# Router on unnormalised rows in halves, row splits on POOL, two sets of transposes moved

## The reference, cut to what matters

```python
# first block
o = o * rsqrt(mean(o * o) + eps)                  # retention, per head
y_ret = (silu(g_ret) * o) @ w_branch_ret
mixed = sigmoid(gate_a) * y_ret + sigmoid(gate_b) * y_lru
h = h + mixed @ w_out
u = rmsnorm(h, ffn_norm_w);  gu = u @ w_ffn_in
# second block
mem_h = _rmsnorm(mem, g_mem);  k = _rmsnorm(mem_h @ w_kv[:, :1024] per head, k_gain)
x = x + merged @ w_out
h = _rmsnorm(x, g_ffn)                            # h = x * rsqrt(mean(x*x)+eps) * g_ffn
g_logits = h @ w_r1 + b_r1;  e_logits = h @ w_r2 + b_r2
g_sel = argmax(g_logits)                          # one of 4 groups per row
# in the group: the best 2 of 4 experts, softmax weights, hidden of 256, summed back
x = x + moe(h)
```

## Time and profile before

| | us |
|---|---|
| median of 3 runs | 1151.18 (1149.7 to 1153.47) |
| profiled execution | 1144.04 |
| its span, first to last instruction | 1142.1 |
| TensorE busy | 1105.1 (97%) |
| VectorE busy | 731.5 (64%) |
| ScalarE busy | 618.5 (54%) |
| POOL busy | 64.8 (6%) |

### The profile page before, as it was taken

How to read it: one execution, slowest core, us unless ns; L and a number is a source line. 1 busy time by engine, 2 the same in 40 slices (tenths; PEclk the granted TensorE clock), 3 DMA queues, 4 the chain that set the end, 5 groups by cost and what they waited for, 6 DMA issues and landing times.

```text
span 1142.1 us, 17273 instructions
## 1 busy us (share of the span) xinstructions
PE 1105.1 (97%) x7128; PEld 980.8 (86%) x7128; DVE 731.5 (64%) x809; ACT 618.5 (54%) x724; POOL 64.8 (6%) x56
## 2 busy tenths in 40 slices
PE   8999999999999999999999999899999989899996
PEld 5998889999878999998897778699999858688885
DVE  6854665865555444546765568956453677988884
ACT  7543479662455344434645355854434357777772
POOL 0410200000100000000000000000011100000140
PEclk9999999999999999999999999999999999999998
DMA  8552254654554555554454434234555535899891
GB/s 305 171 187 88 75 189 164 238 174 159 207 206 156 188 188 196 195 194 147 147 190 143 148 111 148 78 144 148 197 185 182 187 148 181 332 355 350 323 347 63
DMA packets 30468, 215.07 MB, mean 188 GB/s; under 512 B 3377, under 2 KB 3505, under 8 KB 4929
## 3 DMA queue, kind: packets, MB, share of 16 engines
q1 hardware_dynamic: 28112, 199.61, 49.5%
q0 software_dynamic: 1872, 13.11, 3.0%
q10 hardware_dynamic: 416, 1.39, 0.3%
HBM read 213.04 MB, written 1.05 MB: 187 GB/s over the span
## 4 chain that ended last, share of the span: by engine, by line
PE 86%; DVE 8%; ACT 3%; issue 1%; DMA 0%; POOL 0%; DVEq 0%; SPq 0%; ACTq 0%; POOLq 0%
PE bank L526 26%; PE bank L528 26%; PE bank L527 26%; DVE wlo L1511 1%; ACT buf L1040 1%; PE bank L1014 1%; PE bank L587 1%; PE bank L939 1%; DVE wlo L1508 1%; ACT whi L1040 1%; PE bank L900 1%; PE bank L882 1%; DVE normedT_lo L1535 0%; PE bank L651 0%; DMA buf<-x_dram 0%
## 5 line engine op out<-in xcount | busy, mean ns | idle before, releaser
L1511 DVE TENSOR_TENSOR wlo<-raw,whi 128x2048 fp32r<-128x2048 f32 x139 | 320.7, 2312 | 213.6 <-ACT whi L1040 213.3
L1040 ACT ACTIVATE whi<-raw 128x2048 fp32r<-128x2048 f32 x168 | 320.8, 1915 | 140.4 <-PE bank L528 140.1
L1040 ACT ACTIVATE buf<-bank 128x512 f32<-128x512 f32 (+5 forms) x167 | 78.8, 510 | 192.1 <-PE bank L528 171.4
L526 PE MATMUL bank<-normedT_hi,whi 128*128 128x256 f32 x640 | 179.2, 280 | 3.3 <-DVE normedT_lo L1535 3.3
L527 PE MATMUL bank<-normedT_lo,whi 128*128 128x256 f32 x640 | 178.3, 279 | 0.0
L528 PE MATMUL bank<-normedT_hi,wlo 128*128 128x256 f32 x640 | 178.2, 278 | 0.0
L526 PE MATMUL bank<-xT_hi,whi 128*128 128x256 f32 (+1 forms) x448 | 127.8, 285 | 3.2 <-DVE xT_lo L1556 3.2
L528 PE MATMUL bank<-xT_hi,wlo 128*128 128x256 f32 (+1 forms) x448 | 127.6, 285 | 0.0
L527 PE MATMUL bank<-xT_lo,whi 128*128 128x256 f32 (+1 forms) x448 | 127.4, 284 | 0.0
L526 PEld LDWEIGHTS bank<-normedT_hi,whi 128*128 128x128 f32 x640 | 120.9, 189 | 4.5 <-issue 4.1
L528 PEld LDWEIGHTS bank<-normedT_hi,wlo 128*128 128x128 f32 x640 | 121.5, 190 | 0.0
(11 more groups left out here) (383 smaller groups left out, 2277.0 us busy)
## 6 DMA issues: line engine op xcount, KB each, us to landing
raw<-weights_dram SPq DMA_DIRECT2D x168, 1024.0 KB, 4.9
buf<-weights_dram SPq DMA_DIRECT2D x19, 1024.0 KB, 5.1
buf<-x_dram SPq DMA_DIRECT2D x2, 512.0 KB, 4.3
buf<-mem_dram ACTq DMA_DIRECT2D x1, 1024.0 KB, 9.7
out_dram<-buf SPq DMA_DIRECT2D x2, 512.0 KB, 3.0
buf<-final_w_dram POOLq DMA_DIRECT2D x1, 512.0 KB, 3.9
con<-consts_dram SPq DMA_DIRECT2D x1, 486.0 KB, 10.0
buf<-small_w_dram SPq DMA_DIRECT2D x1, 432.0 KB, 12.5
```

The source lines that it names most:

```text
L526: E.matmul(out_, lh, rh, start=start, stop=False)
L1040: return S.activation(out_, in_, func, **kw)
L1511: V.tensor_tensor(wlo[:, n % SLOTS, :], raw[:, n % SLOTS, :], whi[:, n % SLOTS, :].bitcast(f32), sub).then_inc(piece_split, 1)
```

## The change

- The router's weights in `small_w` are multiplied by `gffn` once at the start. X itself is turned (`turn_out`) and split without scale or gain; each row's scale is applied to its 20 logits where the bias is added.
- X is added, squared and turned by column half c and row block r: t3.0 and t3.1 (the left half) are turned between out2's matmuls, t3.2 and t3.3 behind them, the latter between router matmuls. The right half's router matmuls are made for 128 rows at a time. The 28 spins are gone, 3 of 10 before the gather too. A small `Sqrt` and a small `Exp` (`heated`) load ScalarE's tables earlier.
- POOL takes over the split of the second expert piece and both `zrows_lo`. The split of the third expert piece on VectorE moves behind the index.
- The subtraction of the maxima and the choice of the group's expert logits move behind PICK.
- The banks of t3, rl, xa and xb change, and expert_up(0) waits only for the xa that it reads.
- `tr` is turned ahead of gate_b's last piece, `tm` behind br_ret, `th` between the halves of mem_k, with their splits on ScalarE and VectorE; the wait for banks 0 to 3 stands ahead of the first down product of the feed-forward.
- Seven semaphores for square roots become one that counts.

```diff
-_fill(*_n("g", 2, 2), *_n("lg", 2, KT), *_n("lgate", 4), *_n("ga", 4), *_n("gb", 4))
-_fill(*_n("tm", 4), *_n("tr", 4), *_n("br", 4), *_n("bl", 4), *_n("out1", 2, 2), *_n("mk", 2, 2), *_n("th", 4))
+_fill(*_n("g", 2, 2), *_n("lg", 2, KT), *_n("lgate", 4), *_n("ga", 4), "gb.0", "gb.1", "gb.2")
+_fill(*_n("tr", 4), "gb.3", *_n("br", 4), *_n("tm", 4), *_n("bl", 4), *_n("out1", 2, 2))
+_next = 0
+_fill(*_n("mk.0", 2))
+_next = 4
+_fill(*_n("th", 4))
+_next = 2
+_fill(*_n("mk.1", 2))
...
-_fill(*_n("out2", 2, 2), *_n("t3", 4))
-_next = 3
+_fill(*_n("out2", 2, 2), "t3.0", "t3.1", "t3.2")
+_next = 0
 _fill("rlT")
+_next = 7
+_fill("t3.3")
+_next = 1
+_fill("rl", "cum", "xa.0", "xa.1", "xa.2")
 _next = 0
-_fill("rl", "cum")
-_next = 4
-_fill(*_n("xa", 4))
-_next = 1
+_fill("xa.3")
...
                     sp.wait_ge(xn_split, RT)
-                    sp.wait_ge(turned, turns["t3.3"])
...
+            for j in range(3):
+                cols_product(PB["gate_b"] + j, XT, [f"gb.{j}"], first=META)
+            pe.wait_ge(o_ready, 1)
+            turn_rows("tr", O)
+            cols_product(PB["gate_b"] + 3, XT, ["gb.3"], first=META)
             for j in range(4):
-                cols_product(PB["gate_b"] + j, XT, [f"gb.{j}"], first=META)
+                cols_product(PB["br_ret"] + j, RTP, [f"br.{j}"], ready=None if j else after_turn("tr"))
             pe.wait_ge(normed["mem"], RT)
             turn_rows("tm", MR)
-            pe.wait_ge(o_ready, 1)
-            turn_rows("tr", O)
-            for j in range(4):
-                cols_product(PB["br_ret"] + j, RTP, [f"br.{j}"], ready=None if j else after_turn("tr"))
             pe.wait_ge(low["lru"], 1)
             for j in range(4):
                 cols_product(PB["br_lru"] + j, LTP, [f"bl.{j}"])
             for c in range(2):
                 rows_product(PB["out1"] + 2 * c, MIXP, _n(f"out1.{c}", 2), TT, None if c else after_parts(low["mix"]))
             moved(pe, *_n("tm", 4))
-            for c in range(2):
-                rows_product(PB["mem_k"] + 2 * c, MTP, _n(f"mk.{c}", 2), TT)
+            rows_product(PB["mem_k"], MTP, _n("mk.0", 2), TT)
             pe.wait_ge(normed["h"], RT)
             turn_rows("th", XN)
+            rows_product(PB["mem_k"] + 2, MTP, _n("mk.1", 2), TT)
...
+            def turn_out(c, r):
+                moved(pe, f"out2.{c}.{r}")
+                turn(f"t3.{2 * c + r}", [(k * P, X[:, r, (4 * c + k) * P:(4 * c + k + 1) * P]) for k in range(4)])
+
             for c in range(2):
-                rows_product(PB["out2"] + 2 * c, MRGP, _n(f"out2.{c}", 2), TT, None if c else after_parts(low["merge"]))
-            turn_rows("t3", XN, (28, 0, 0, 0), (normed["z"], RT))
-
+                outs = [begin(x) for x in _n(f"out2.{c}", 2)]
+                for half in range(2):
+                    w = [part.rearrange("p (k c) -> p k c", k=4) for part in piece(PB["out2"] + 2 * c + half)]
+                    for r in range(RT):
+                        if c == 1 and half == 0 and r == 1:
+                            turn_out(0, 0)
+                            turn_out(0, 1)
+                        for k in range(4):
+                            if c == 0 and r == 0 and k % 2 == 0:
+                                pe.wait_ge(low["merge"], 2 * half + k // 2 + 1)
+                            last = product(outs[r][:, :], both(MRGP, ALL, 4 * half + k, slice(r * P, (r + 1) * P)), both(w, ALL, k),
+                                           half == 0 and k == 0, half == 1 and k == 3)
+                        if c == 1 and half == 1 and r == 0:
+                            last.then_inc(out_row, 1)
+                    last.then_inc(pieces_used, 1)
+
+            def routed(b, k, lo, hi):
+                (lh, ll), (rh, rl) = both(SW, ALL, k, slice(88, 108)), both(HTP, ALL, k, slice(lo, hi))
+                out_ = b[0:20, lo:hi]
+                E.matmul(out_, lh, rh, start=k == 0, stop=False, skip_group_check=True)
+                E.matmul(out_, lh, rl, start=False, stop=False, skip_group_check=True)
+                return E.matmul(out_, ll, rh, start=False, stop=k == KT - 1, skip_group_check=True)
+
+            turn_out(1, 0)
             b = begin("rlT")
-            for k in range(KT):
-                after_turn("t3")(k)
-                last = product(b[0:20, 0:T], both(SW, ALL, k, slice(88, 108)), both(HTP, ALL, k), k == 0, k == KT - 1)
+            moved(pe, "t3.0", "t3.1")
+            routed(b, 0, 0, T)
+            routed(b, 1, 0, T)
+            turn_out(1, 1)
+            routed(b, 2, 0, T)
+            routed(b, 3, 0, T)
+            for r in range(RT):
+                moved(pe, f"t3.{2 + r}")
+                for k in range(4, KT):
+                    last = routed(b, k, r * P, (r + 1) * P)
...
-                    spin(b, 10)
+                    spin(b, 7)
...
-                        if p == 0 and half == 0 and k == 0:
-                            moved(pe, "xa.2")
...
+                if j == 3:
+                    turned_high("tr", RTP[0])
                 full(act, PB["gate_b"] + j + 1)
                 release(A(GB[:, 2 * j:2 * j + 2, :], bank(f"gb.{j}")[:, :].rearrange("p (k t) -> p k t", k=2), ACT.Sigmoid), f"gb.{j}")
+            for j in range(4):
+                feed(act, PB["br_ret"] + j + 2)
             turned_high("tm", MTP[0], W("gmem"))
-            turned_high("tr", RTP[0])
             for j in range(4):
...
-            full(act, PB["out2"] + 4)
-            moved(act, *_n("out2", 2, 2))
-            row_squares("z", X)
-            row_roots("z")
-            act.wait_ge(z_scale, 1)
-            for r in range(RT):
+            feed(act, PB["out2"] + 3)
+            A(heated, stat["y"][:, 0:1], ACT.Sqrt)
+
+            def z_squares(c, r):
+                moved(act, f"out2.{c}.{r}")
+                cs = slice(c * 512, (c + 1) * 512)
+                A(XN[:, r, cs], X[:, r, cs], ACT.Square, scale=1.0 / 32, accum_out=zss[:, r, c:c + 1]).then_inc(squares, 1)
+
+            def z_root(r):
+                act.wait_ge(meansq, nth["z"] + r)
+                A(stat["z"][:, r:r + 1], stat["z"][:, r:r + 1], ACT.Sqrt).then_inc(rooted, 1)
+
+            def z_rows_high(r):
+                act.wait_ge(z_scale, r + 1)
                 A(XNS[0][:, r, :], X[:, r, :], ACT.Copy, scale=stat["z"][:, r:r + 1]).then_inc(xn_high, 1)
-            turned_high("t3", HTP[0], W("gffn"))
-            feed(act, M0 + 2)
+
+            def z_turned_high(c, r):
+                act.wait_ge(turned, turns[f"t3.{2 * c + r}"])
+                A(HTP[0][:, 4 * c:4 * c + 4, r * P:(r + 1) * P], bank(f"t3.{2 * c + r}")[:, :].rearrange("p (k t) -> p k t", k=4), ACT.Copy).then_inc(high["t3"], 1)
+
+            feed(act, M0)
+            z_squares(0, 0)
+            z_squares(0, 1)
+            z_turned_high(0, 0)
+            z_turned_high(0, 1)
+            feed(act, M0 + 1)
+            z_squares(1, 0)
+            z_root(0)
+            z_rows_high(0)
+            z_turned_high(1, 0)
+            z_turned_high(1, 1)
+            z_squares(1, 1)
+            z_root(1)
             act.wait_ge(route_part, 1)
             release(A(RLW, bank("rlT")[0:20, 0:T], ACT.Copy), "rlT")
+            z_rows_high(1)
+            A(heated, stat["z"][:, 0:1], ACT.Exp)
...
+            router = SWR.rearrange("p (k c) -> p k c", k=KT)[:, :, 88:108]
+            V.tensor_tensor(router, router, bc(W("gffn"), 20), mult).then_inc(small_scaled, 1)
...
+                if j == 0:
+                    turned_low("tm", MTP, W("gmem"))
...
-            head_sums([(f"mk.{c}.{r}", c, r, PB["mem_k"] + 2 * c + 2) for c in range(2) for r in range(RT)], MSQ, mkss, 2, mk_summed)
+            head_sums([(f"mk.0.{r}", 0, r, PB["mem_k"] + 2) for r in range(RT)], MSQ, mkss, 2, mk_summed)
+            turned_low("th", HTP, W("ffnw"))
+            head_sums([(f"mk.1.{r}", 1, r, PB["mem_k"] + 4) for r in range(RT)], MSQ, mkss, 2, mk_summed)
             head_mean(mkss, 256, mk_summed, 4)
-            turned_low("th", HTP, W("ffnw"))
...
+            def z_sum(c, r):
+                cs = slice(c * 512, (c + 1) * 512)
+                release(V.tensor_tensor(X[:, r, cs], X[:, r, cs], bank(f"out2.{c}.{r}")[:, :], add), f"out2.{c}.{r}")
+
+            def z_turned_low(c, r):
+                dve.wait_ge(high["t3"], 2 * c + r + 1)
+                hi, lo = (part[:, 4 * c:4 * c + 4, r * P:(r + 1) * P] for part in HTP)
+                release(V.tensor_tensor(lo, bank(f"t3.{2 * c + r}")[:, :].rearrange("p (k t) -> p k t", k=4), hi.bitcast(f32), sub), f"t3.{2 * c + r}")
+
+            def z_mean(r):
+                dve.wait_ge(squares, squares_ahead["z"] + RT + r + 1)
+                V.scalar_tensor_tensor(stat["z"][:, r:r + 1], zss[:, r, 0:1], EPS, zss[:, r, 1:2], add, add).then_inc(meansq, 1)
+
+            def z_scales(r):
+                s = stat["z"][:, r:r + 1]
+                dve.wait_ge(rooted, nth["z"] + r)
+                V.reciprocal(s, s).then_inc(z_scale, 1)
```

(57 more changed lines are left out.)

85 lines of the change are left out of this document (41 added, 44 removed).

## The result

| | before | after |
|---|---|---|
| median (us) | 1150.44 (1149.6 to 1153.47, 4 runs) | 1135.09 (1134.64 to 1136.28, 4 runs) |
| profiled execution | 1144.04 | 1135.47 |
| span, mean granted clock | 1142.1, 0.994 | 1133.6, 0.989 |

The ratio of the medians is 0.9866, with a 95% interval of 0.9832 to 0.99: 15.4 us less. The two profiled executions differ by 8.6 us, near the forecast's sum of 9.2.

A forecast was written before the change was run, and what follows sets the result against it. TensorE, busy for 97% of the span, was taken as the bound, so only its waits could give time back. 1.9 + 3.3 + 4.8 - 0.8 = 9.2 gave 1134.8 profiled; with 7.1 added back, 1142.0 median, range 1136.8 to 1146.4.

The forecast's parts named there:

- the median is 7.1 above the profiled execution, and I add that back: Whole kernel: the runs' median 1151.18 against the profiled 1144.04; 7.1 us added to 1134.8, giving 1142.0.
- the clock rival: Routing to first expert: half-clock falls over spins, gather and first expert cost 3.2 us, hence 1144.4; chance 0.15.
- Part 1: Retention: transposes moved ahead of gate_b's last piece remove a TensorE wait; gain 1.9 us, bounds 0.7 and 1.9.
- Part 2: Feed-forward: transposes moved between mem_k's halves remove a TensorE wait; gain 3.3 us, bounds 2.9 and 3.3.
- Routing: From out2's end to the first expert: a shorter path without idle matmuls; gain 4.8 us, bounds 4.5 and 5.2.
- both holds of 2.2 and 2.1: Routing: POOL's subtracts delay VectorE's `z_mean` by 2.2 us and its two-operand index steps by 2.1.
- the first expert's 0.98: Ahead of the first expert: TensorE's idle 0.98 us goes, since it no longer waits for bank 6 (xa.2).
- The 0.7 us for VectorE's moved split: Between index and copy of the shares: the third expert piece's split loses up to 0.7 us of the gain.
- The clock: Routing and gather without spins: a possible half-clock fall loses 0.8 us, bounds 0 and 1.6.
- POOL's splits did not hide: Routing: the rival said tiny VectorE operations slip past POOL, returning 2.2 + 2.1 us, hence 1137.7; chance 0.22.
- The experts: Expert stage: the rival said VectorE and loads pace it, so the 4.8 us shrinks to nothing, hence 1146.0; chance 0.08.
- The steady half clock: Routing, gather and first experts: without the 28 spins the clock stays at half, making the kernel slower; chance 0.03.

The follow-up runs named there:

- f4: The unchanged kernel before, profiled a third time and not timed beside another; the execution took 1155.14 us at clock 0.981.
- e1: The unchanged kernel before, profiled once more and timed again: median 1149.38 us, ratio 0.9972; its profiled execution took 1149.49.
- e6: The changed kernel with `z_mean` written to read one SBUF tensor and take the other sum as a per-partition scalar: median 1138.19 us.
- the filled pair: The kernels before and after, both with idle matmuls on zeros in TensorE's waits: medians 1144.71 and 1132.73 us.
- e5: The kernel before with 14 idle matmuls in the wait ahead of the feed-forward: median 1150.92 us, ratio 0.9989.
- g1: The kernel before with idle matmuls on zeros in six waits of TensorE: median 1144.71 us, ratio 0.9939.
- g2: The changed kernel with idle matmuls in the same six waits, but for the two it does not have: median 1132.73 us, ratio 0.9845.

## Why the prediction was wrong, by its own steps
- **The step that failed is "the median is 7.1 above the profiled execution, and I add that back".** It took the 7.1 for something that does not depend on the kernel. The first profile was one of the fastest executions that before has, with two falls of the clock ahead of the end; f4, at 1155.14 and the most common clock, has eight, which make all of its 11.1 us more, and e1 has four and the slower pace in the feed-forward. The change removed waits behind which the clock falls, and the offset did not come with it: after's median, 1135.09, equals its profiled execution, 1135.47. Leaving the step out, the same sum says 1134.8, which looks right, but by luck: it compares an unusually good execution of before with a typical one of after. Between typical executions the change gives 15.4 to 16.6 us, and the sum had 9.2.
- **What misled it.** It held against the clock rival that behind the 3.3 us idle ahead of the feed-forward the clock did not fall. That was one execution; in four of five profiles with this wait unfilled it did fall there, at a cost of 2.5 us in f4. A wait was priced at its length alone.
- **Part 1** (1.9 forecast). Right in mechanism; the wait went. br_lru's products end 2.8 us earlier (294.69 to 291.89), because retention's 192 products also ran at 0.1133 instead of 0.1179 us (0.9), which the sum did not have.
- **Part 2** (3.3). The wait went. The sum had no term for the bank that mem_k takes over from out1: from out1's start to mem_k's are 1.25 us more (0.98 of them the wait), and from there to the feed-forward 3.55 less (27.39 to 23.84). With part 1 that makes the 5.1 at the feed-forward.
- **Routing** (4.8, less 0.8 for the clock). POOL's 4.6 and 2.4, both holds of 2.2 and 2.1 (2.3 and 2.1 measured) and the first expert's 0.98 came as written; the first expert starts 18.6 us behind out2's end, forecast 18.5. The 0.7 us for VectorE's moved split did not come.
- **The clock** (-0.8). The sign was wrong. It did fall ahead of the gather, at 922, but in place of the fall at 948, which had cost 1.5. Over many executions the median clock rose from 0.984 to 0.9885; at 0.74 us per 0.001 that is 3.3 us of the 16.6 between the pooled medians (94 and 10 executions), and at an equal clock of 0.99 the lines are 13.2 apart. Ten executions are few: e6, the changed kernel with one operation written otherwise, has a median clock of 0.984, as before.
- **The rivals.** POOL's splits did not hide (2.45 and 2.26 us). The clock was in the path, but of the kernel before. The experts gave back nothing but 1.6 at 972 and 1.9 from 1119 on, both with a fall of the clock. The steady half clock did not come.

What stays open: what decides in which execution a wait brings the clock down, how much of the 6.8 us comes from falls and how much from the pace of the products, and how the 12.0 of the filled pair and the 13.2 at equal clock come apart.

## What to carry to other kernels
Before a sum is made against a profiled execution, look where that execution lies among the timed ones and at what clock; an offset between the two is a term of its own, and the change may take it away. A wait of TensorE can cost more than its length, since dense products behind it ran at half clock for 3.4 or 6.8 us in many of the executions here; where waits could not be removed, matmuls on zeros in six of them gave 7.5 us. And work handed to POOL is not off VectorE's path if it reads SBUF while VectorE has two-operand steps, however small: two of three subtracts back in VectorE's idle moments gave 2.8 us.

## What the runs showed of the hardware
- The same products of 256 columns, at a granted clock of 1.0, run at one of two paces, 0.1133 or 0.1179 us, mostly through a whole stage. In e1's feed-forward it was the slower throughout, 4.2 us in 165; in e5's it was the slower up to about 376 and the faster from there on, with the clock at 1.0. Count of matmuls in 16 us, before's first profile, e1, and e5 behind its change of pace:

```profile
386.00:402.00 16.00, 16.00 (x120) 15.10 (x119) 8.17 (x5) 6.36 (x5) 0.00 (x0) 1.00 0.57 191
```

```profile
386.00:402.00 16.00, 16.00 (x116) 14.99 (x115) 7.44 (x6) 6.75 (x5) 0.00 (x0) 1.00 0.57 198
```

```profile
386.00:402.00 16.00, 16.00 (x119) 15.02 (x119) 7.86 (x6) 6.76 (x5) 0.00 (x0) 1.00 0.58 197
```

In twelve profiles with the moved transposes both retention and feed-forward had the faster one; in seven with the old order, retention had the slower in three and the feed-forward in one, besides e5's first part. br_lru's 192 products had the slower pace in all twelve with the new order, and retention's pace, whichever it was, in the seven with the old. So the order of the program has a part in it; what sets the pace was not found.
- A one-column VectorE operation with two SBUF operands waits until POOL's instruction ends (0.15 becomes 2.45); one with an operand in PSUM does not wait (0.69 in the middle of POOL's 4.6).
- The clock fell behind waits as short as 2.1 and 1.0 us with a few transposes between them (724), and at 104 in g1 and g2 behind small products with no wait at all. Each fall lasted 3.4 or 6.8 us and cost 0.8 to 2.8 us where dense work stood behind it.
